# Narrower scores for the first 128 queries of the causal attentions

## What is computed

```python
s = jnp.einsum('bqhd,bkhd->bhqk', q_i, k) * scale      # 128 queries of block i, 256 keys
s = jnp.where(kpos[None, :] <= qpos[:, None], s, -jnp.inf)
p = jax.nn.softmax(s, axis=-1)
o = jnp.einsum('bhqk,bkhv->bqhv', p, v)
```

## Time and profile before

| | |
|---|---|
| runs | 2942.96, 2943.32, 2943.55 us; median 2943.32 |
| the profiled execution | 2943.0 us, its span 2941.2 us |
| mean granted TensorE clock | 0.98 |
| PE busy | 2783.1 us, 95% |
| DVE busy | 1537.9 us, 52% |
| ACT busy | 468.8 us, 16% |
| POOL busy | 104.0 us, 4% |
| DMA | 454.98 MB, mean 155 GB/s |

### The profile page before, as it was taken

One profiled execution on the slowest core, in us unless ns is written; L12 is line 12 of the kernel. 1 busy time (PEld: TensorE's weight loads), 2 busy tenths in 40 slices (PEclk: granted clock), 3 DMA queues, 4 the chain that ended last, 5 costly groups with the idle time before them and its releaser, 6 DMA issues.

```text
span 2941.2 us, 38976 instructions
## 1 busy us (share of the span) xinstructions
PE 2783.1 (95%) x16254; PEld 2495.0 (85%) x16254; DVE 1537.9 (52%) x3064; ACT 468.8 (16%) x823; POOL 104.0 (4%) x88
## 2 busy tenths in 40 slices
PE   3999999989999999999989999998889999988998
PEld 3899889878889999888868999876778998877888
DVE  4457675453547766465553566434235652222565
ACT  1001332411100100242221100012110011111000
POOL 0000000000000330000000240000000000000000
PEclk7999999999999999999999999998999999989999
DMA  7887521223787444431123444432324444322442
GB/s 288 303 297 274 222 90 58 86 101 140 274 303 276 159 168 164 144 121 65 58 100 112 161 172 164 152 115 86 115 92 151 158 158 151 115 96 98 155 148 99
DMA packets 73440, 454.98 MB, mean 155 GB/s; under 512 B 8112, under 2 KB 8880, under 8 KB 27440
## 3 DMA queue, kind: packets, MB, share of 16 engines
q1 hardware_dynamic: 73120, 451.44, 42.7%
q0 software_dynamic: 144, 1.05, 0.1%
HBM read 451.41 MB, written 1.05 MB: 154 GB/s over the span
## 4 chain that ended last, share of the span: by engine, by line
PE 92%; DVE 4%; issue 1%; DMA 1%; DVEq 1%; ACT 0%; SPq 0%; ACTq 0%
PE psum L506 21%; PE psum L460 20%; PE psum L615 14%; PE psum L555 9%; PE psum L754 7%; PE psum L835 4%; PE psum L674 3%; PE psum L698 2%; PE psum L570 2%; PE psum L774 2%; PE psum L686 1%; PE psum L482 1%; PE psum L721 1%; PE psum L711 1%; PE psum L932 1%
## 5 line engine op out<-in xcount | busy, mean ns | idle before, releaser
L460 PE MATMUL psum<-h,ring 128*128 128x256 f32 x1776 | 391.3, 382 | 22.7 <-issue 20.2
L460 PEld LDWEIGHTS psum<-h,ring 128*128 128x128 f32 x1776 | 340.1, 192 | 73.4 <-issue 23.1
L506 PE MATMUL psum<-h,ring 128*128 128x256 f32 x1376 | 298.9, 380 | 29.9 <-ACT h L1054 29.9
L506 PEld LDWEIGHTS psum<-h,ring 128*128 128x128 f32 x1376 | 262.4, 191 | 66.2 <-issue 30.3
L506 PE MATMUL psum<-aring,ring 128*128 128x256 f32 x1408 | 304.7, 379 | 1.7 <-issue 1.7
L506 PEld LDWEIGHTS psum<-aring,ring 128*128 128x128 f32 x1408 | 267.4, 190 | 38.7 <-issue 2.4
L615 PE MATMUL psum<-arena 128*128 128x128 f32 x2112 | 249.6, 275 | 0.0
L615 PEld LDWEIGHTS psum<-arena 128*128 128x128 f32 x2112 | 242.6, 192 | 0.0
L754 PE MATMUL psum<-h,ring 128*128 128x256 f32 x1024 | 232.2, 383 | 0.0
L754 PEld LDWEIGHTS psum<-h,ring 128*128 128x128 f32 x1024 | 194.1, 192 | 27.2 <-issue 1.9
L615 PE MATMUL psum<-arena,ring 128*128 128x128 f32 x1584 | 191.6, 275 | 0.0
(11 more groups left out here) (396 smaller groups left out, 3391.6 us busy)
## 6 DMA issues: line engine op xcount, KB each, us to landing
ring<-wstream SPq DMA_DIRECT2D x354, 1024.0 KB, 4.8
aring<-astream SPq DMA_DIRECT2D x134, 512.0 KB, 5.0
ring<-astream SPq DMA_DIRECT2D x10, 512.0 KB, 13.3
kst<-const SPq DMA_DIRECT2D x1, 1344.5 KB, 10.2
x<-xT SPq DMA_DIRECT2D x1, 1024.0 KB, 7.4
arena<-memT POOLq DMA_DIRECT2D x1, 1024.0 KB, 5.6
outT<-h SPq DMA_DIRECT2D x1, 1024.0 KB, 3.9
condb<-crow SPq DMA_DIRECT2D x1, 512.0 KB, 5.3
```

Of the source, the lines that this page charges most:

```text
L460: mm = pe.matmul(out, lhsT=tile_at(at[0] % RING, t), rhs=rhs(k), start=k == 0, stop=k == kt - 1)
L506: mm = pe.matmul(psum[:, s % 4, n * T:(n + 1) * T], lhsT=tile_at(slot, n * KD + k), rhs=rhs(k), start=k == 0, stop=k == KD - 1)
```

## The change

For the causal kinds, tile t = 0 gets width 128 in place of 256 in all steps in which it still had 256: the scores, scale and mask, the subtraction of fox, the maximum, the exponential and its sum, the normalising. Tile t = 1 keeps 256, and so do both tiles of "mem". Where DVE had one instruction over both tiles (2 x 256 elements: L1702, L1696, L1705, L1707) there are now two, of 128 and of 256 elements. No wait, drain or DMA is added or removed.

```diff
+        def width(kind, t):
+            return T if kind == "mem" or t else P
...
-                                    mm = pe.matmul(psum[:, i % 2 * 2 + m, t * T:(t + 1) * T],
-                                                   lhsT=qs[a][:, t * P:(t + 1) * P], rhs=ks[a],
+                                    w = width(kind, t)
+                                    mm = pe.matmul(psum[:, i % 2 * 2 + m, t * T:t * T + w],
+                                                   lhsT=qs[a][:, t * P:(t + 1) * P], rhs=ks[a][:, 0:w],
                                                    start=a == 0, stop=a == len(qs) - 1)
...
-                                src = LB[:, b, m, t]
+                                dst = src = LB[:, b, m, t, 0:width(kind, t)]
                                 if kind == "mem":
                                     src = psum[:, b * 2, t * T:(t + 1) * T]
-                                last = E(LB[:, b, m, t], src, ACT.Exp, bias=col(NM, b * 4 + m * 2 + t),
+                                last = E(dst, src, ACT.Exp, bias=col(NM, b * 4 + m * 2 + t),
...
-                        if kind == "mlstm":
-                            TT(dst, mask, sq[:, i:i + 1].broadcast_to((P, 2, T)), ALU.add)
-                        elif kind == "mla":
-                            for t in range(2):
-                                STT(out=dst[:, t], in0=s[:, t], scalar=col(RQ, 8 * t + i), in1=mask[:, t], op0=ALU.mult,
-                                    op1=ALU.add)
-                        else:
-                            STT(out=dst, in0=s, scalar=scale, in1=mask, op0=ALU.mult, op1=ALU.add)
+                        for t in range(2):
+                            w = width(kind, t)
+                            d, k, z = dst[:, t, 0:w], mask[:, t, 0:w], s[:, t, 0:w]
+                            if kind == "mlstm":
+                                TT(d, k, sq[:, i, 0:w], ALU.add)
+                            elif kind == "mla":
+                                STT(out=d, in0=z, scalar=col(RQ, 8 * t + i), in1=k, op0=ALU.mult, op1=ALU.add)
+                            else:
+                                STT(out=d, in0=z, scalar=scale, in1=k, op0=ALU.mult, op1=ALU.add)
                         D()
                         if kind == "fox":
-                            TT(dst, dst, sq[:, i:i + 1].broadcast_to((P, 2, T)), ALU.subtract)
+                            for t in range(2):
+                                w = width(kind, t)
+                                TT(dst[:, t, 0:w], dst[:, t, 0:w], sq[:, i, 0:w], ALU.subtract)
                             D()
-                        V.tensor_reduce(col(MX, b * 4 + 2 * m, 2), dst, AXX, ALU.max)
+                        for t in range(2):
+                            V.tensor_reduce(col(MX, b * 4 + 2 * m + t, 1), dst[:, t, 0:width(kind, t)], AXX, ALU.max)
...
                         for t in range(2):
-                            TS(LB[:, b, 1, t], LB[:, b, 1, t], col(RC, b * 4 + 2 + t), None, ALU.mult)
+                            v = LB[:, b, 1, t, 0:width(kind, t)]
+                            TS(v, v, col(RC, b * 4 + 2 + t), None, ALU.mult)
                         D()
                     for t in range(2):
                         r = col(RC, b * 4 + t)
+                        w = width(kind, t)
+                        v = LB[:, b, 0, t, 0:w]
                         if kind == "diff":
-                            last = STT(out=LB[:, b, 0, t], in0=LB[:, b, 0, t], scalar=r, in1=LB[:, b, 1, t],
-                                       op0=ALU.mult, op1=ALU.subtract)
+                            last = STT(out=v, in0=v, scalar=r, in1=LB[:, b, 1, t, 0:w], op0=ALU.mult, op1=ALU.subtract)
                         else:
-                            last = TS(LB[:, b, 0, t], LB[:, b, 0, t], r, None, ALU.mult)
+                            last = TS(v, v, r, None, ALU.mult)
```

More of the change, by code:

```diff
@@ L1732, in normalise @@
                         for t in range(2):
-                            STT(out=LB[:, b, 0, t], in0=psum[:, b * 2, t * T:(t + 1) * T], scalar=scale,
-                                in1=LB[:, b, 0, t], op0=ALU.mult, op1=ALU.mult, accum_out=col(SM, b * 4 + t))
+                            w = width(kind, t)
+                            STT(out=LB[:, b, 0, t, 0:w], in0=psum[:, b * 2, t * T:t * T + w], scalar=scale,
+                                in1=LB[:, b, 0, t, 0:w], op0=ALU.mult, op1=ALU.mult, accum_out=col(SM, b * 4 + t))
                         D()
```

## The result

| | before | after |
|---|---|---|
| runs | 4: 2942.96 to 2943.55 us | 4: 2923.86 to 2925.35 us |
| median | 2943.27 us | 2924.43 us |
| profiled execution | 2943.0 us, span 2941.2 | 2925.35 us, span 2923.6 |

The ratio is 0.9936, with a 95% interval of 0.9924 to 0.9948: 18.8 us faster, where 13.6 were forecast. The direction is right, the size is not.

What follows compares the result with a forecast made beforehand. PE, busy 95% of the span, was taken to bound the kernel. PE's 10.9 us plus DVE's 2.6 us gave 13.5 us off 2943.3: 2929.8, say 2929.7 us; forecast's own range 2926.5 to 2932.7.

Steps and rivals of the forecast that it cites:

- Narrow scores, PE: Score matmuls in mla, fox, diff and mlstm: each narrowed record saves 0.103 us of PE, together 10.9 us.
- first head: In mlstm, running at the lower clock: its two narrowed score records save 0.21 us each, 0.42 us.
- Splitting DVE instructions: DVE in the attentions: a pair of 128 and 256 takes 0.627 us against 0.69; DVE's part 2.6 us.
- rival A: Split DVE instructions cost their full fixed part, fox's wait stays whole: gain 11.35 us, 2932.0 us; chance 0.15.
- Fox's wait: PE's wait for DVE before fox's transposes: DVE's chain shrinks 0.26 us a head, returning 1.8 us over 7 heads.
- Rival B: Weight loads of 0.19 us limit the 104 narrow score records: 8.0 us less, gain 5.5, 2937.8 us; chance 0.06.
- Rival C: Weight stream behind layer 0's mla takes back at most that attention's 3.4 us: 2933.2 us; chance 0.04.
- Rival D: PE granted the lower clock in the mla attentions, 46 us for a whole attention: 2975 us; chance 0.03.
- the clock: PE's 1.2 GHz stretches after gaps: left out of the sum, some 2 us per full recovery, 3 us allowed.

Runs made afterwards that it cites:

- scores_only: Kernel before with only the score matmuls of the first query tile narrowed, mask, maximum, exponential and normalising left at 256; 2934.07 us, ratio 0.9967.
- before_look1: Kernel before, unaltered, profiled again; span 2944.0 us.
- after_again: Changed kernel, unaltered, run and profiled again; 2927.32 us, ratio 0.9943.
- before_pad2: Kernel before with two memsets, each with a drain, on DVE's list ahead of the first modulation and norm; 2943.93 us, ratio 0.9999.
- after_pad2: Changed kernel with two memsets, each with a drain, on DVE's list ahead of the first modulation and norm; 2927.35 us, ratio 0.9946.
- after_pad4: Changed kernel with four memsets, each with a drain, on DVE's list ahead of the first modulation and norm; 2927.82 us, ratio 0.9945.
- before_warm: Kernel before with dummy matmuls in PE's pauses, 8 behind diff and 9 behind mlstm; 2938.57 us, ratio 0.9981.
- after_warm: Changed kernel with dummy matmuls in PE's pauses, 8 behind diff and 9 behind mlstm; 2924.62 us, ratio 0.9934.

## Why the prediction missed

- **Narrow scores, PE: right.** 0.105 us for each narrowed record (forecast 0.103). mla 3.34 us per layer in scores_only (forecast 3.30), 3.40 in after with the 0.07 of the last head (3.37). Fox 1.7, from the heads of scores_only, each 0.21 us shorter, though a low-clock stretch took that back in its profile. Diff 1.7 (1.65). Mlstm 0.6 for the last three heads as forecast. Its first head is the small miss: in the profile that I read it ran at 1.2 GHz and the chain's piece of its four score records was 2.07 us; in before_look1 it was 1.13 and in after 0.92. The narrowing is worth 0.21, not 0.42.
- **Splitting DVE instructions: right, and rival A falls.** Pairs of 0.61 to 0.63 us against 0.69; the maximum, which no row had shown, behaves like the rest. The Trainium skill ("VectorE: DVE Perf Modes", section "The TRN2 errata — SBUF-src ops pay a fixed extra latency per instruction") advises against small tiles, since each instruction pays the latency anew. In this case's traces 128 elements fewer outweigh one more instruction, by 0.06 to 0.08 us a pair, as the overlap in the earlier trace rows had it. Fox's wait fell from 3.5 us to 1.9 in total; the whole of fox gave 3.3 against a forecast of 1.65 + 1.8, and 3.6 in the two profiles without the new stall.
- **Rival B (weight loads bound narrow records): falls.** The pitch of a narrow record is 1.31 / 4 less 0.216, 0.11 us, though its load takes 0.19.
- **Rival C (weight stream): falls.** The DMA queue waits 129.4 us for DVE from 745 to 900 us, where it waited 127.3; both layers keep their 3.40 us.
- **Rival D (lower clock in mla): falls.** The mla heads have 3.45 us of filler and 1.31 of scores, 0.42 us less than before in each.
- **The step that failed: the clock.** The sum left the recoveries after PE's pauses out and "allowed 3 us" to each side. Two things were wrong in it. The allowance was too small: in the table the columns behind pauses differ by up to 4 us between kernels (2572: -2.5 to 1.6), and two profiles of one kernel by 1.7 us in one column (fox) or by 2.4 (after and after_again at 2572). And it wasn't centred: the profile I read was the fastest of four, 1.7 us below their mean, and low levels and stalls that an edit upstream can dissolve or make were priced at nothing. In the recorded pair of profiles this step was worth 4.0 us net, in the means of four 4.5 us. The profiled executions lie 17.6 us apart; the other 1.2 us of the 18.8 are the spread between executions.
- **Small slips, of no weight.** The sum gives 2929.8 and the text says 2929.7; 3 us below that is 2926.7 and not 2926.5.

The mean of the four profiles of after against that of before, column by column: the attentions give 6.8 + 3.3 + 2.7 + 0.6 and 0.2 for mlstm's first head, 13.6 us. That is the forecast's sum, with two stalls in it that cancel: 0.4 us won in diff, 0.3 lost in fox. Beside them 1949 gives 1.7, fox's first heads at the full clock 1.3, 2050 1.3, the stall at 1654 0.4, 2500 0.5 and the part up to 1650 0.5, together 5.7; 2572 takes 0.8 and the part up to 2500 0.4. That is 18.1, the 18.1 of the spans.

Of these, the stalls that went (0.8 with diff's), 1949 (1.7) and fox's first heads (1.3) are shown to come without any narrower score: before_pad2 has them all. That the narrowing has them only because it shifts instructions on DVE's list and pauses in time is argued, not shown. The 1.8 us at the head sums of 2050 are absent in after_pad2 and after_pad4, which have the whole change; before_warm doesn't explain it, since its own gain there lies behind the pause and that of after ahead of it. What decides between 3.47 and 5.16 us at 1949, and between 1.95 and 3.75 us at 2050, stays open, as do the 0.5 us up to 1650, where the weights first stream in and the four profiles of after themselves differ by 1.8.

## What to carry to other kernels

A change of 0.5% can be summed from the chain to within 0.2 us where the engine is dense, but its time is that sum plus what happens at the engine's pauses, which here moved by up to 2.4 us at a single place between two profiles of one kernel. Before forecasting, take several profiles of the same kernel, and put the spread of the stretches behind pauses into the range, not the spread of the runs. What a change is worth by itself is read from its own stretches, record by record. A second pair of whole kernels doesn't tell it: the plain pair differed by 18.8 us, the padded ones by 16.6 and 14.7 and the one with filled pauses by 13.95, each with another set of stretches at the lower clock.

## What the runs showed of the hardware

- A stall of 0.43 to 0.45 us between two DVE instructions, with no wait that the profile shows, was in 7 of 7 profiles with one list of DVE instructions ahead of it and in none of 11 with another. Every profile has 6 to 13 such stalls, always at the same instructions of one kernel. In this study edits upstream both removed them (0.43 us at 1654) and made them (0.41 us in fox).
- After the same pause, the same 16 matmuls took 5.16 or 3.47 us by the granted clock, the same way in the four profiles of before and in the four of after, but otherwise in a kernel with two memsets more at its start.
- Memsets that moved the kernel before's work by 1.5 and 2.8 us at the start cost nothing measurable at the end (ratios 0.9999 and 0.9996).
- The kernel before with dummy matmuls in two pauses was 5.8 us faster, 4.3 us of it in the two stretches with dummies. With 3.2 us of the second pause left empty, the projection behind it ran at a granted clock of 1.00 in before_warm and of 0.67 in after_warm.
